# The mLSTM head stage of a two-layer decoder trunk, with the next iteration's projections dealt between its steps

## The chip, the cores and the metric

One NeuronCore of one Trainium2 chip runs the whole program, two layers, in one launch. The metric is device time in microseconds, the median of several executions. One further execution was taken with the hardware profiler, and all rows below come from it.

## What is computed

Each layer adds a token mixer and an expert feed-forward to x (512 tokens by 1024 columns, float32). The mixer has three branches that read column groups of one projection of the normalised x: an RG-LRU, a forgetting attention, and an mLSTM; each is projected, gated and summed ("merged"). The change touches the third branch:

```python
q, k, v = 8 heads of 128 columns each, of xn @ w_in;  i, f = 8 gate columns each
b = cumsum(log_sigmoid(f));  d[t, s] = b[t] - b[s] + i[s] for s <= t;  m[t] = running maximum
w[t, s] = exp(d[t, s] - m[t]) * (q[t] . k[s]) / sqrt(128)
h[t] = sum_s w[t, s] v[s] / max(|sum_s w[t, s]|, exp(-m[t]))
hc = h - mean(h);  y = hc / sqrt(mean(hc * hc) + eps) * norm_w * sigmoid(o)
merged += sigmoid(gate_c) * (y @ w_br_mlstm)
```

## The kernel before

Every dense projection is made with split float32: POOL turns a weight slot of 128 by 1024 (loaded by SP's DMA into one of four ring buffers) into a rounded high part `w_hi` and a remainder `w_lo` (`split_parts`, L610 to L616), each in one of two buffers; TensorE then sums 24 products of 512 columns, 16 with the high activations (L727) and 8 with the low ones (L730), into bank s of four (`project`). ScalarE or VectorE empties the bank. A round is four slots. `proj_done`, `split_ready` and the `drained` semaphores tie them together. Each engine runs its own program strictly in its written order, and waits on semaphores.

A layer goes through LRU, forgetting attention (FQ), values (MV), merge (MB), output gates (MO), then the mLSTM head stage (**MQ**, four iterations), merge (MC), output projection, normalisation, and the experts (UE, VE), which take the second half. In FQ the next round's projection is already dealt between the steps of attention by a generator, `project_beside`: `next()` on it issues `step` products.

An MQ iteration handles two heads, p = 0 and 1. In the kernel before it is a hardware loop (`Fori`) on each engine:

- **TensorE** projects the iteration's queries and keys (slots 0 to 3: q0, k0, q1, k1). After slots 1 and 2 it spreads the gate rows of head 0 and 1 over all partitions (L922; G to bank 6, M to bank 7), with selectors that POOL writes (`sel`, L664). When all four banks are empty: scores of both heads (L931, banks 4 and 5, four key blocks each), numerator and denominator of head 0 (L942), mean of head 0 (L950), numerator and denominator of head 1, then mean square of head 0, mean of head 1, mean square of head 1 (L950).
- **ScalarE** copies queries and keys (L1241), copies G (L1251), makes the floor exp(-m) (L1254) and, behind VectorE's mask, the decays E (L1261, L1263); later the numerator's copy (L1268), squares (L1272, L1237), square roots (L1279), and the high part of y (L1281).
- **VectorE** adds the mask (L1654), multiplies scores into decays (`weigh`, L1664), takes the larger of denominator and floor (L1675, L1677), centres (L1683), adds up the variance (L1700), then for each head reciprocal (L1703) and two products (L1705, L1707), and last the low part of y (`low_part`, L1491).
- **POOL** splits slots 0 and 1, writes `sel`, copies the iteration's two heads of values into a buffer `vst` (L669), from which the numerator's weights are loaded, and splits slots 2 and 3.

`fill_wait` makes TensorE wait until a bank's last contents are taken; `filled` and `drained` count per phase and iteration. The merge MC then runs four rounds; slots 0 and 1 of a round (gates) read xn, slots 2 and 3 read y, so slot 2 of its first round waits for y's low part. `stand` increments a semaphore that nothing waits on.

Of the kernel before, what the change touches and what calls it, by code (L numbers as in the profile page):

```python
# [11 lines left out]
ALU = mybir.AluOpType  # L12
ACT = mybir.ActivationFunctionType
AX = mybir.AxisListType
ds = bass.ds

P = 128
# [131 lines left out]

def build(nc, x_in, w_stream, w_lru, pvec, nrows, fnorm, u_tab, v_tab, out):  # L150
# [3 lines left out]
    with ExitStack() as ctx:  # L154
# [76 lines left out]
        vst = sb("vst", [P, TT, 2, P])  # L231
# [70 lines left out]
        pickw = vst[:, 0, 0, :]  # L302
# [79 lines left out]
        vst_ready = Count(sem("vst_ready"), dict(MQ=(4, 1)))  # L382
# [42 lines left out]
        def loaded(L, phase, i):  # L425
            return 16 * (L * NLOAD + i + LOAD0[phase]) + 16

# [137 lines left out]
        def _(pool):  # L565
# [68 lines left out]
            with pool.Fori(0, DEPTH) as L:  # L634
# [24 lines left out]
                with pool.Fori(0, 4) as i:  # L659
                    split_round(L, "MQ", i, (0, 1))  # L660
                    pool.wait_ge(filled[7].sem, filled[7].at(L, "MQ", i, 0))
                    pool.wait_ge(filled[6].sem, filled[6].at(L, "MQ", i, 0))
                    stand(pool)
                    nc.gpsimd.tensor_copy(sel[:, 0:2, :], head_hot[:, ds(2 * i, 2)]  # L664
                                          .unsqueeze(2).to_broadcast([M_AT + ML_H, 2, P])).then_inc(sel_ready.sem, 1)
                    for s in range(4):
                        pool.wait_ge(drained[s].sem, drained[s].at(L, "MV", 1, 1))
# [3 lines left out]
                    split_round(L, "MQ", i, (2, 3))  # L671
# [27 lines left out]
        def _(pe):  # L699
# [45 lines left out]
            def project_beside(L, ph, i, x, step):  # L745

                for s in range(4):
# [56 lines left out]
            def merge(L, ph, hi, branch_out):  # L804


                stand(pe)
                with pe.Fori(0, 4) as i:
                    for s in range(4):
                        if s == 2:  # L810
                            pe.wait_ge(y_lo_ready.sem, y_lo_ready.at(L, *branch_out, 1))
                        project(L, ph, i, s, x_parts(xl_mix) if s < 2 else y_parts(hi))

            with pe.Fori(0, DEPTH) as L:
# [101 lines left out]
                with pe.Fori(0, 4) as i:  # L916
                    n = {6: 0, 7: 0}

                    def spread(b, p, at):
                        fill_wait(b, L, "MQ", i, n[b])  # L920
# [4 lines left out]
                        n[b] += 1  # L925

                    def scores_of(p):
                        for s in range(TT):
                            b = 4 + s % 2
                            fill_wait(b, L, "MQ", i, 2 * p + s // 2)  # L930
                            nc.tensor.matmul(bank[b][:, 0:SEQ - s * P], qk[:, 2 * p + 1, s * P:(s + 1) * P],  # L931
                                             qk[:, 2 * p, s * P:SEQ], start=True, stop=True)\
                                .then_inc(filled[b].sem, 1)

                    def num_den(p):
                        for b in (6, 7):
                            fill_wait(b, L, "MQ", i, n[b])
                            for s in range(TT):
                                if b == 6:
                                    pe.wait_ge(wts_ready.sem, wts_ready.at(L, "MQ", i, 4 * p + s + 1))  # L940
                                lhsT = vst[:, s, p, :] if b == 6 else ones[:, 0:P]
                                mm = nc.tensor.matmul(bank[b][:, s * P:SEQ], lhsT, E[:, p, s, 0:SEQ - s * P],  # L942
                                                      start=(s == 0), stop=(s == TT - 1))
                            mm.then_inc(filled[b].sem, 1)
                            n[b] += 1

                    def mean(p, b, src, ready):
                        pe.wait_ge(ready.sem, ready.at(L, "MQ", i, p + 1))
                        fill_wait(b, L, "MQ", i, n[b])
                        nc.tensor.matmul(bank[b][:, :], inv[:, :], src[:, p, :], start=True, stop=True)\  # L950
                            .then_inc(filled[b].sem, 1)
                        n[b] += 1


                    for s in range(4):
                        project(L, "MQ", i, s, x_parts(xl_mix))
                        if s == 1:
                            pe.wait_ge(sel_ready.sem, sel_ready.at(L, "MQ", i, 1))
                        if s in (1, 2):
                            spread(6, s - 1, G_AT)  # L960
                            spread(7, s - 1, M_AT)
                    for s in range(4):
                        pe.wait_ge(drained_sem[s], drnd(L, "MQ", i) + 2)
                    pe.wait_ge(vst_ready.sem, vst_ready.at(L, "MQ", i, 1))
                    scores_of(0)
                    scores_of(1)
                    num_den(0)
                    mean(0, 6, hh, h_ready)
                    num_den(1)
                    mean(0, 7, sq, hsq_ready)  # L970
                    mean(1, 6, hh, h_ready)
                    mean(1, 7, sq, hsq_ready)
                merge(L, "MC", y_hi, ("MQ", 3))
# [110 lines left out]
        def _(act):  # L1084
# [39 lines left out]
            with act.Fori(0, DEPTH) as L:  # L1124
# [109 lines left out]
                with act.Fori(0, 4) as i:  # L1234
                    def centred_square(p):
                        act.wait_ge(hc_ready.sem, hc_ready.at(L, "MQ", i, p + 1))
                        nc.scalar.activation(sq[:, p, :], hh[:, p, :], ACT.Square).then_inc(hsq_ready.sem, 1)  # L1237

                    for s in range(4):
                        proj_wait(L, "MQ", i, s)  # L1240
                        nc.scalar.activation(qk[:, s, :], bank[s][:, :], ACT.Copy,  # L1241
                                             scale=ML_D ** -0.5 if s % 2 == 1 else 1.0)\
                            .then_inc(drained_sem[s], 1)
                        if s in (1, 2):

                            p = s - 1
                            act.wait_ge(filled[6].sem, filled[6].at(L, "MQ", i, p + 1))
                            if p == 1:

                                act.wait_ge(dec_ready.sem, dec_ready.at(L, "MQ", i, TT))  # L1250
                            nc.scalar.copy(gb, bank[6][:, :]).then_inc(drained_sem[6], 1)  # L1251
                            act.wait_ge(filled[7].sem, filled[7].at(L, "MQ", i, p + 1))
                            act.wait_ge(ml_y.sem, ml_y.at(L, "MQ", i, p) - 1)
                            nc.scalar.activation(em[:, p, :], bank[7][:, :], ACT.Exp, scale=-1.0)\  # L1254
                                .then_inc(drained_sem[7], 1)
                            act.wait_ge(drained_sem[6], drained[6].at(L, "MQ", i, p + 1))
                            act.wait_ge(gdm_ready.sem, gdm_ready.at(L, "MQ", i, p + 1))
                            for k in range(TT):
                                gs = gcol[:, k, ds(2 * i + p, 1)]
                                if k < TT - 1:  # L1260
                                    nc.scalar.activation(E[:, p, k, P:SEQ - k * P], gb[:, (k + 1) * P:], ACT.Exp,  # L1261
                                                         scale=-1.0, bias=gs)
                                nc.scalar.activation(E[:, p, k, 0:P], gdm[:, k, :], ACT.Exp, scale=-1.0, bias=gs)\  # L1263
                                    .then_inc(dec_ready.sem, 1)
                    for p in range(2):

                        act.wait_ge(filled[6].sem, filled[6].at(L, "MQ", i, 3 + 2 * p))
                        nc.scalar.copy(hh[:, p, :], bank[6][:, :]).then_inc(drained_sem[6], 1)  # L1268
                        act.wait_ge(drained_sem[6], drained[6].at(L, "MQ", i, 3 + 2 * p))
                        act.sem_inc(h_ready.sem, 1)  # L1270
                        act.wait_ge(drained_sem[7], drained[7].at(L, "MQ", i, 3 + p))
                        nc.scalar.activation(em[:, p, :], em[:, p, :], ACT.Square, scale=EPS ** 0.5)\  # L1272
                            .then_inc(dsq_ready.sem, 1)
                        if p == 1:
                            centred_square(0)
# [118 lines left out]
        def _(dve):  # L1394
# [102 lines left out]
            with dve.Fori(0, DEPTH) as L:  # L1497
# [375 lines left out]
                def one_hots(k, s):  # L1873
# [5 lines left out]
                    if k % 8 == 0 and s == 0:  # L1879
                        V.tensor_copy(pickw, pickT[:, 2, :])  # L1880
# [206 lines left out]
```

## Time and profile before

| | us |
|---|---|
| median of 3 runs | 4980.68 |
| lowest, highest | 4971.8, 4984.4 |
| profiled execution | 4974.69 |
| its span | 4972.8 |

Head stages in the profiled span: from 690 to 920 in the first layer, 3170 to 3390 in the second. The profile's chain of waits follows the work that ended last backwards; its pieces, given with a start and a duration, are the work and the waits on which the end depended. In the timeline of an engine, the number in brackets behind a row is the idle time ahead of it and the instruction that ended it. TensorE's products are pipelined, so a product's duration is longer than the spacing to the next. A float32 product that is not split shows as two records.

### The profile page before, as it was taken

The page shows a single profiled execution, that of the slowest core. Times are in us where ns is not written, and L with a number is a line of the kernel's source. Part 1 is how long each engine was busy: PE and PEld are TensorE (multiplying, and loading weights), DVE is VectorE, ACT ScalarE, POOL GpSimd, SP SyncE. Part 2 cuts the span into 40 slices and gives each one's busy share as a digit, 9 for nine tenths or more (in the row PEclk, how much of TensorE's full clock was granted, in tenths as well). Part 3 has the DMA queues.
Part 4 walks back from the last instruction along what each step waited for, and adds up shares of the span by engine and source line. Part 5 has one row for each costly group of instructions (what it writes and reads, how often), then busy time and mean ns, then how long its engine had stood idle before and what let it go on. Part 6 is the DMA issues. An engine that isn't in the chain of part 4 may idle for free.

```text
span 4972.8 us, 73478 instructions
## 1 busy us (share of the span) xinstructions
PE 4465.8 (90%) x21194; PEld 3693.0 (74%) x21194; DVE 3182.8 (64%) x5031; ACT 1763.7 (35%) x3198; POOL 2740.8 (55%) x1485
## 2 busy tenths in 40 slices
PE   6899998889989887999878999989898889879998
PEld 4666775679888886777756667757798888867776
DVE  7434225338889775888883352343488897668888
ACT  2234213213555652333222341231145556523332
POOL 5643664565455664555456436636554566645554
PEclk9999999999999998999989999999999999989999
DMA  2211221224578999999722112212246889989996
GB/s 96 68 60 39 73 76 42 68 76 127 179 243 265 293 303 317 337 341 331 276 67 70 56 39 81 72 42 74 72 141 188 243 263 303 303 301 342 338 331 251
DMA packets 463118, 893.00 MB, mean 180 GB/s; under 512 B 41376, under 2 KB 320416, under 8 KB 459808
## 3 DMA queue, kind: packets, MB, share of 16 engines
q1 hardware_dynamic: 387424, 617.22, 38.4%
q0 software_dynamic: 73728, 268.47, 15.8%
q10 hardware_dynamic: 1728, 4.89, 0.3%
q14 instruction: 180, 1.47, 0.1%
q8 instruction: 58, 0.95, 0.1%
HBM read 787.65 MB, written 102.76 MB: 179 GB/s over the span
## 4 chain that ended last, share of the span: by engine, by line
PE 54%; DVE 19%; DMA 10%; issue 9%; ACT 4%; SPq 2%; DVEq 1%; POOL 1%; ACTq 0%; POOLq 0%
DMA ring<-v_tab 7%; PE pair L727 6%; PE bank L727 6%; PE bank L1062 5%; PE bank L1067 5%; PE bank L1057 4%; PE bank L1005 3%; PE pair L730 3%; PE bank L730 3%; DMA ring<-u_tab 3%; PE bank L880 2%; PE bank L753 2%; DVE ring L1849 2%; PE bank L794 2%; DVE qk L1882 2%
## 5 line engine op out<-in xcount | busy, mean ns | idle before, releaser
L613 POOL TENSOR_TENSOR w_hi<-ring,ones 128x1024 fp32r<-128x1024 f32 x272 | 546.7, 2010 | 857.1 <-PE bank L730 291.3
L601 POOL TENSOR_TENSOR w_lo<-ring,w_hi 128x1024 fp32r<-128x1024 f32 x256 | 634.2, 2478 | 552.3 <-ACT w_hi L1304 545.8
L1005 PE MATMUL bank<-xT,w_hi 128*128 128x384 f32 x2048 | 728.0, 355 | 24.7 <-ACT gst L1316 21.2
L616 POOL TENSOR_TENSOR w_lo<-ring,w_hi 128x1024 fp32r<-128x1024 f32 x272 | 696.9, 2562 | 21.3
L1005 PE MATMUL bank<-xl_peer,w_hi 128*128 128x384 f32 x2048 | 705.3, 344 | 0.0
L1310 ACT CAST w_hi<-ring 128x1024 fp32r<-128x1024 f32 x256 | 269.7, 1053 | 719.5 <-PE bank L1067 440.9
L1304 ACT CAST w_hi<-ring 128x1024 fp32r<-128x1024 f32 x256 | 268.9, 1050 | 637.7 <-DVE ring L1849 496.6
L1941 DVE TENSOR_TENSOR cl<-att,ch 128x384 fp32r<-128x384 f32 x256 | 356.8, 1394 | 213.8 <-ACT ch L1375 206.8
L607 POOL TENSOR_TENSOR w_lo<-ring,w_hi 128x1024 fp32r<-128x1024 f32 x128 | 306.6, 2395 | 316.7 <-ACT w_hi L1310 316.6
L1057 PE MATMUL bank<-w_hi,ch 128*128 128x512 f32 x1536 | 395.4, 393 | 53.4 <-ACT ch L1375 53.3
L1005 PEld LDWEIGHTS bank<-xT,w_hi 128*128 128x128 f32 x2048 | 402.5, 197 | 28.4 <-ACT w_hi L1304 18.8
L1062 PE MATMUL bank<-w_hi,cl 128*128 128x512 f32 x1536 | 396.6, 394 | 20.2 <-DVE cl L1941 19.9
L1005 PEld LDWEIGHTS bank<-xl_peer,w_hi 128*128 128x128 f32 x2048 | 402.1, 196 | 0.3 <-issue 0.3
L1009 PE MATMUL bank<-xT,w_lo 128*128 128x384 f32 x2048 | 398.0, 335 | 0.0
L1067 PE MATMUL bank<-w_lo,ch 128*128 128x512 f32 x1536 | 390.4, 389 | 0.0
L1057 PEld LDWEIGHTS bank<-w_hi,ch 128*128 128x128 f32 x1536 | 287.7, 189 | 122.6 <-ACT w_hi L1310 60.6
L1009 PEld LDWEIGHTS bank<-xT,w_lo 128*128 128x128 f32 x2048 | 359.4, 188 | 0.8 <-POOL w_lo L601 0.8
L1062 PEld LDWEIGHTS bank<-w_hi,cl 128*128 128x128 f32 x1536 | 287.6, 189 | 93.4 <-DVE cl L1941 33.8
L1036 PE MATMUL bank<-qk 128*128 128x128 f32 x1536 | 223.2, 291 | 140.1 <-ACT qk L1332 139.1
L727 PE MATMUL bank<-xT,w_hi 128*128 128x512 f32 (+1 forms) x816 | 329.7, 404 | 17.6 <-POOL w_lo L616 10.4
L1067 PEld LDWEIGHTS bank<-w_lo,ch 128*128 128x128 f32 x1536 | 288.7, 188 | 60.6
L1036 PEld LDWEIGHTS bank<-qk 128*128 128x128 f32 x1536 | 202.9, 200 | 167.1 <-issue 166.7
(322 smaller groups left out, 9184.4 us busy)
## 6 DMA issues: line engine op xcount, KB each, us to landing
ring<-v_tab SPq DMA_DIRECT2D x256, 512.0 KB
ring<-w_stream SPq DMA_DIRECT2D x240, 512.0 KB
ring<-u_tab SPq DMA_DIRECT2D x512, 128.0 KB
g_spill<-gst SPq DMA_DIRECT2D x256, 192.0 KB
hn<-u_tab SPq DMA_DIRECT2D x256, 128.0 KB
x_last<-u_tab SPq DMA_DIRECT2D x256, 128.0 KB
w_spill<-vg SPq DMA_DIRECT2D x12, 2048.0 KB, 8.9
w_spill<-att SPq DMA_DIRECT2D x12, 2048.0 KB
```

Source lines behind the costliest of these rows:

```text
L601: nc.gpsimd.tensor_tensor(w_lo[s % 2][:, :], ring[2 + s % 2][:, :], w_hi[s % 2][:, :].bitcast(F32), ALU.subtract)\
L607: nc.gpsimd.tensor_tensor(w_lo[s % 2][:, :], ring[s][:, :], w_hi[s % 2][:, :].bitcast(F32), ALU.subtract)\
L613: nc.gpsimd.tensor_tensor(w_hi[b][:, 0:n], src, ones[:, 0:1].to_broadcast([P, n]), ALU.mult)\
L616: nc.gpsimd.tensor_tensor(w_lo[b][:, 0:n], src, w_hi[b][:, 0:n].bitcast(F32), ALU.subtract)\
L727: nc.tensor.matmul(out, w(c)[part], x(c)[0], start=(c == 0 and part == 0), stop=False)
L1005: nc.tensor.matmul(out, w_hi[s % 2][:, c * P:(c + 1) * P], dense_parts(c)[part], start=(c == 0 and part == 0), stop=False)
L1009: mm = nc.tensor.matmul(out, w_lo[s % 2][:, c * P:(c + 1) * P], dense_parts(c)[0], start=False, stop=(c == KC - 1))
L1036: mm = nc.tensor.matmul(bank[b][:, j * P:(j + 1) * P], hot2[s % 2][:, j, :], hot1[s % 2][:, j, :], start=True, stop=True)
L1057: nc.tensor.matmul(bank[acc[2 * t + h]][:, :], ch[s % 2][:, cols[t]], w_hi[s % 2][:, halves[h]], start=start, stop=False)
L1062: nc.tensor.matmul(bank[acc[2 * t + h]][:, :], cl[s % 2][:, cols[t]], w_hi[s % 2][:, halves[h]], start=False, stop=False)
L1067: mm = nc.tensor.matmul(bank[acc[2 * t + h]][:, :], ch[s % 2][:, cols[t]], w_lo[s % 2][:, halves[h]], start=False, stop=stop)
L1941: V.tensor_tensor(cl[s % 2][:, :], cf[s % 2], ch[s % 2][:, :].bitcast(F32), ALU.subtract)\
```

## The change

TensorE, ScalarE and POOL run the four iterations unrolled; VectorE runs three in a loop and the last one apart. During iteration i TensorE issues iteration i + 1's projection in pieces of six products (four per slot), and its gate rows singly, between iteration i's steps. In the last iteration the pieces are slots 0 and 1 of MC's first round, and MC then begins with its slots 2 and 3. Counts on banks 6 and 7 follow two written-out lists of fills. ScalarE's and VectorE's steps are put in a new order. The numerator reads its weights from `v_sb` itself; `vst` goes, and `pickw`, which lay in it, gets a buffer of its own.

```diff
+FILLS = {6: ["G00", "G01"], 7: ["M00", "M01"]}
+for _i in range(4):
+    _next = _i < 3
+    FILLS[6] += [f"num{_i}0", f"h{_i}0", f"num{_i}1"] + [f"G{_i + 1}0"] * _next + [f"h{_i}1"] + [f"G{_i + 1}1"] * _next
+    FILLS[7] += [f"den{_i}0", f"den{_i}1", f"q{_i}0", f"q{_i}1"] + [f"M{_i + 1}0", f"M{_i + 1}1"] * _next
...
         @block.gpsimd
-                    nc.gpsimd.tensor_copy(vst[:, :, :, :].rearrange("p t a n -> p t (a n)"),
-                                          v_sb[:, :, ds(2 * P * i, 2 * P)]).then_inc(vst_ready.sem, 1)
...
+                for i in range(1, 4):
+                    pool.wait_ge(filled[6].sem, sums(filled, L, f"G{i - 1}1"))
+                    pool.wait_ge(filled[7].sem, sums(filled, L, f"M{i - 1}1"))
                     stand(pool)
+                    gate_rows(i)
+                    split_round(L, "MQ", i)
...
         @block.tensor
+                            lhsT = v_sb[:, s, at:at + P] if b == 6 else ones[:, 0:P]
...
+                for i in range(4):
+                    if i < 3:
+                        beside = project_beside(L, "MQ", i + 1, x_parts(xl_mix), 6)
+                        share = [4, 2, 2, 2, 3, 3]
+                    else:
+                        beside = project_beside(L, "MC", 0, x_parts(xl_mix), 6, range(2))
+                        share = [4, 1, 1, 1, 1, 0]
+
+                    def dense():
+                        for _ in range(share.pop(0)):
+                            next(beside)
+
+                    scores_of(i, 0)
+                    scores_of(i, 1)
+                    dense()
+                    num_den(i, 0)
+                    dense()
+                    mean(i, 0, f"h{i}0", hh, h_ready)
+                    num_den(i, 1)
+                    dense()
+                    if i < 3:
+                        pe.wait_ge(sel_ready.sem, sel_ready.at(L, "MQ", i + 1, 1))
+                        spread(i + 1, 0)[0]()
+                    dense()
+                    mean(i, 0, f"q{i}0", sq, hsq_ready)
+                    mean(i, 1, f"h{i}1", hh, h_ready)
+                    dense()
+                    mean(i, 1, f"q{i}1", sq, hsq_ready)
+                    if i < 3:
+                        spread(i + 1, 0)[1]()
+                    dense()
+                    if i < 3:
+                        for one in spread(i + 1, 1):
+                            one()
+                    beside.close()
+                merge(L, "MC", y_hi, ("MQ", 3), 1)
...
         @block.scalar
+                for i in range(4):
+                    if i < 3:
+                        query_key(i + 1, 0)
+                    numerator(i, 0)
+                    floor_square(i, 0)
+                    numerator(i, 1)
+                    if i < 3:
+                        query_key(i + 1, 1)
+                        decay_row(i + 1, 0)
+                    centred_square(i, 0)
+                    floor_square(i, 1)
+                    if i < 3:
+                        decays(i + 1, 0)
+                        query_key(i + 1, 2)
+                    centred_square(i, 1)
+                    deviation(i, 0)
+                    deviation(i, 1)
+                    if i < 3:
+                        floors(i + 1, 0)
+                        query_key(i + 1, 3)
+                        decay_row(i + 1, 1)
+                        decays(i + 1, 1)
+                        floors(i + 1, 1)
                     act.wait_ge(ml_y.sem, ml_y.at(L, "MQ", i, 2))
+                    nc.scalar.copy(y_hi[:, 2 * i:2 * i + 2, :], yT[:, 2 * i:2 * i + 2, :]).then_inc(y_hi_ready.sem, 1)
...
         @block.vector
+                decay_mask(0, 0)
+                decay_mask(0, 1)
+                def heads(i, more):
                     c = Chain(dve, dve_step, L, "MQ", i)
+                    weigh(i, 0)
+                    weigh(i, 1)
+                    denominator(c, i, 0)
+                    centre(i, 0)
+                    denominator(c, i, 1)
+                    if more:
+                        decay_mask(i + 1, 0)
+                    centre(i, 1)
+                    variance(i, 0)
+                    variance(i, 1)
                     for p in range(2):
                         dve.wait_ge(dev_ready.sem, dev_ready.at(L, "MQ", i, p + 1))
                         c.step(V.reciprocal(em[:, p, :], em[:, p, :]))
...
+                    if more:
+                        decay_mask(i + 1, 1)
                     c.close()
                     low_part(L, "MQ", i, y_lo, yT, y_hi, 1)
...
+                with dve.Fori(0, 3) as i:
+                    heads(i, True)
+                heads(3, False)
```

`numerator`, `floor_square`, `centred_square`, `deviation`, `decay_row`, `decays`, `floors` and `query_key` are the same instructions as before, each now a function. `floors(i + 1, p)` waits until y of head p of iteration i is done, `decays` for the mask, `decay_row` of head 1 for head 0's decays.

## Rows read from the trace of the kernel before

**Rows 1.** The page: busy time of each engine, with share and instructions
```profile
PE 4465.8 (90%) x21194; PEld 3693.0 (74%) x21194; DVE 3182.8 (64%) x5031; ACT 1763.7 (35%) x3198; POOL 2740.8 (55%) x1485
```

**Rows 2.** Windows: busy us by engine, then PEclk, DMA share, GB/s
```profile
769.67:823.11 53.44, 44.02 (x161) 28.89 (x161) 26.11 (x25) 17.40 (x33) 19.76 (x11) 0.97 0.12 39
823.11:877.59 54.48, 45.31 (x161) 29.45 (x161) 26.11 (x25) 17.41 (x33) 19.74 (x11) 0.94 0.11 40
877.59:920.49 42.90, 32.65 (x105) 20.09 (x105) 22.38 (x23) 9.38 (x13) 9.98 (x5) 0.92 0.08 30
...
925.00:960.00 35.00, 35.00 (x155) 29.01 (x154) 11.84 (x10) 4.76 (x5) 27.23 (x12) 1.00 0.27 90
```

**Rows 3.** Chain of waits: start, us, what; last row in the second layer
```profile
776.76 4.34 PE bank L942 x16
...
783.27 4.59 PE bank L942 x16
...
790.62 1.99 PE bank L950 x4
...
794.47 1.14 PE bank L950 x2
...
796.33 3.35 DVE att L1703
...
805.58 2.55 DVE big L1707
...
831.25 4.34 PE bank L942 x16
...
3388.28 1.55 DVE y_lo L1491
```

**Rows 4.** Timeline of VectorE across the loop's end
```profile
800.59 0.69 DVE L1707 TENSOR_TENSOR big<-att,vg 128x512 f32 x1 [0.19 <-DVE att L1705]
...
809.43 1.86 DVE L1491 TENSOR_TENSOR y_lo<-big,y_hi  x1 [1.31 <-ACT y_hi L1281]
812.22 1.89 DVE L1654 TENSOR_TENSOR att<-att,mask_k 128x512 f32<-128x512 f32 x1 [0.93 <-ACT att L1251]
...
825.38 0.69 DVE L1664 TENSOR_TENSOR att<-bank,att 128x512 f32<-128x512 f32 x1 [5.80 <-PE bank L931]
```

**Rows 5.** Chain of waits: two slots in a row of the merge MC
```profile
954.99 3.63 PE bank L727 x16
960.43 3.63 PE bank L727 x16
```

**Rows 6.** Timeline of TensorE: a pair of gate rows spread
```profile
808.06 0.73 PE L922 MATMUL bank<-row_parts,sel 8*128 8x512 f32 x4
```

**Rows 7.** Timeline of ScalarE: y's high part, and the last decays of head 0
```profile
808.26 1.05 ACT L1281 CAST y_hi<-big  x1 [11.18 <-DVE big L1707]
...
816.11 0.68 ACT L1263 ACTIVATE att<-att,gcol 128x128 f32<-128x128 f32 x2
```

**Rows 8.** Timeline of VectorE at the stage's end
```profile
914.53 2.54 DVE L1707 TENSOR_TENSOR big<-att,vg 128x512 f32 x1 [0.26 <-DVE att L1705]
```

**Rows 9.** Timeline of POOL: value copy and splits
```profile
796.39 1.04 POOL L669 COPY vst<-vg 128x1024 f32 x1
802.87 1.90 POOL L613 TENSOR_TENSOR w_hi<-ring,ones 128x1024 fp32r<-128x1024 f32 x1 [5.44 <-PE bank L730]
804.85 2.72 POOL L616 TENSOR_TENSOR w_lo<-ring,w_hi 128x1024 fp32r<-128x1024 f32 x1
808.31 1.90 POOL L613 TENSOR_TENSOR w_hi<-ring,ones 128x1024 fp32r<-128x1024 f32 x1 [0.74 <-PE bank L730]
810.28 3.27 POOL L616 TENSOR_TENSOR w_lo<-ring,w_hi 128x1024 fp32r<-128x1024 f32 x1
```

**Rows 10.** Windows of 2 us in the two falls of the clock
```profile
796.00:798.00 2.00, 2.00 (x6) 1.52 (x6) 2.00 (x2) 0.63 (x1) 1.42 (x2) 0.50 0.00 0
...
824.00:826.00 2.00, 2.00 (x4) 0.67 (x2) 0.62 (x1) 0.00 (x0) 1.33 (x1) 0.50 0.00 0
```

More of the change, by code:

```diff
@@ L802, in xl_of_tile, with merge @@
                 return xl_mix[:, t, c * P:(c + 1) * P]
-            def merge(L, ph, hi, branch_out):
+            def merge(L, ph, hi, branch_out, begun=0):
+                if begun:
+                    pe.wait_ge(y_lo_ready.sem, y_lo_ready.at(L, *branch_out, 1))
+                    for s in range(2, 4):
+                        project(L, ph, 0, s, y_parts(hi))
                 stand(pe)
-                with pe.Fori(0, 4) as i:
+                with pe.Fori(begun, 4) as i:
                     for s in range(4):
-                        if s == 2:
+                        if s == 2 and not begun:
                             pe.wait_ge(y_lo_ready.sem, y_lo_ready.at(L, *branch_out, 1))
@@ L935, in num_den @@
[L935 to L961, printed above, removed]
@@ L973, in _, with scores_of @@
-                merge(L, "MC", y_hi, ("MQ", 3))
+                    return (lambda: one(f"G{i}{p}", G_AT)), (lambda: one(f"M{i}{p}", M_AT))
+                def scores_of(i, p):
+                    for s in (2 * p, 2 * p + 1):
+                        pe.wait_ge(drained_sem[s], drnd(L, "MQ", i) + 2)
+                    for s in range(TT):
+                        b = 4 + s % 2
+                        fill_wait(b, L, "MQ", i, 2 * p + s // 2)
+                        nc.tensor.matmul(bank[b][:, 0:SEQ - s * P], qk[:, 2 * p + 1, s * P:(s + 1) * P],
+                                         qk[:, 2 * p, s * P:SEQ], start=True, stop=True)\
+                            .then_inc(filled[b].sem, 1)
@@ new lines, in mean @@
+                def mean(i, p, name, src, ready):
+                    b = FILL[name]
+                    pe.wait_ge(ready.sem, ready.at(L, "MQ", i, p + 1))
+                    sum_wait(name)
+                    nc.tensor.matmul(bank[b][:, :], inv[:, :], src[:, p, :], start=True, stop=True)\
+                        .then_inc(filled[b].sem, 1)
+                for s in range(4):
+                    project(L, "MQ", 0, s, x_parts(xl_mix))
+                    if s == 1:
+                        pe.wait_ge(sel_ready.sem, sel_ready.at(L, "MQ", 0, 1))
+                    if s in (1, 2):
+                        for one in spread(0, s - 1):
+                            one()
@@ L1232, in _ @@
                             .then_inc(drained_sem[s], 1)
[L1234 to L1275, printed above, removed]
-                    centred_square(1)
-                    for p in range(2):
-                        act.wait_ge(drained_sem[7], drained[7].at(L, "MQ", i, 5 + p))
-                        nc.scalar.activation(em[:, p, :], em[:, p, :], ACT.Sqrt).then_inc(dev_ready.sem, 1)
@@ new lines, in deviation @@
+                def deviation(i, p):
+                    act.wait_ge(drained_sem[7], sums(drained, L, f"q{i}{p}"))
+                    nc.scalar.activation(em[:, p, :], em[:, p, :], ACT.Sqrt).then_inc(dev_ready.sem, 1)
+                for s in range(4):
+                    query_key(0, s)
+                    if s in (1, 2):
+                        decay_row(0, s - 1)
+                        floors(0, s - 1)
+                        decays(0, s - 1)
+                for i in range(4):
[21 more added lines that the diff above has]
+                        floors(i + 1, 1)
```

187 lines of the change are left out of this document (107 added, 80 removed).

## The prediction

> **What bounds the kernel now.** The page's totals first [rows 1]: TensorE is busy for 90% of the span, so hiding other work behind it, or filling its holes, looks like the only way on. But the share is an average. The window table of the head stage [rows 2] gives TensorE 44 to 45 us of work in each full iteration of 53.4 to 54.5 us (two of three are shown), at a granted clock of 0.94 to 0.97, and 32.7 of 42.9 us in the last one, while the merge behind it is full (35.00 of 35.00). So each layer has some 9 us of holes per iteration, which the change wants to fill.
>
> What closes an iteration is read in the chain of waits [rows 3]. I count from one iteration's first numerator group (776.76) to the next (831.25): 54.49 us. Numerator and denominator of head 0 take 4.34 us; its mean and centring bring head 1's numerator to 783.27; its groups end 4.59 us later. The next means start at 790.62 (2.76 us after those groups end, waiting for the floor and centred squares), the last variance at 794.47 (1.86 us after the means end). Then VectorE: reciprocal at 796.33, y of head 1 complete at 805.58 + 2.55 = 808.13. From there to the next iteration's first weighing product, 825.38 [rows 4], pass 17.25 us: y's high part, a table load, queries and keys, both heads' masks and decays. Another 5.87 us of scores and weighing reach the next numerator. This is a loop through three engines, and **TensorE is not its limit**. Only the first two projections of an iteration are hidden now: they begin right after the last variance, under the reciprocals.
>
> **The change, part by part.**
> *Dealt pieces.* A slot's projection is 24 products, 5.44 us (960.43 - 954.99 [rows 5]); a piece is a quarter, 1.36 us. In iterations 0 to 2 the shares are 4, 2, 2, 2, 3, 3. TensorE takes its work in order, so a piece is free only where it already waited. Ahead of head 0's numerator: 4 pieces, 5.44 us, and no wait there (the chain goes from the weighing's scores straight into the numerator): +5.44. Ahead of head 0's mean: 2 pieces, no wait: +2.72. Between head 1's denominator and the next means: 2 + 2 pieces and one gate row, half the 0.73 us pair plus some 0.1 of issue, 0.45 [rows 6]: 5.89 against a wait of 2.76: +3.13. Ahead of the last variance: 3 pieces, 4.08, against 1.86: +2.22. The last 3 pieces lie behind it, under the reciprocals, at nothing; without that cover they would be 4.08. The loop's first part is **13.5 us longer**.
> *What leaves the loop.* Queries, keys and head 0's mask and decays of the next iteration are done before y is ready, so the 17.25 us go.
> *What stands in their place.* Here the new order on VectorE matters. `decay_mask(i + 1, 1)` is put behind both heads' final products, and `low_part` behind that, ahead of the next `weigh`. `low_part` waits for `y_hi`, and ScalarE makes `y_hi` only after `decays(i + 1, 1)` and `floors(i + 1, 1)`, which wait for that very mask. So after y: mask, decays, floor, y high, y low, and only then the weighing, on which scores, numerators and all TensorE work queue up. The mask is 0.69 us (a product of the same width without contention [rows 4]) to 1.89 (now); I take 0.69, as POOL may be between splits. Decays with the hand-over: 814.11 to 816.79, 2.7 [rows 4, 7]. Floor 0.5 net, high part 1.05 with 0.13 before it [rows 7]. Low part 1.55 (second layer) to 1.86 [rows 3, 4], I take 1.55, with its 0.12 wait and 0.35 of issue behind it. Sum 7.1.
> Steady iteration: +13.5 - 17.25 + 7.1 = **+3.4**, three per layer: +10.2.
> *Last iteration.* Its shares are 4, 1, 1, 1, 1, 0, the merge's two x-side slots, which now hide under the final reciprocals. +5.44, then +1.36; 2.72 against the 2.76 wait and 1.36 against the 1.86, at nothing: +6.8. At its end no split is left beside VectorE: the last product at 914.53 took 2.54 against 0.69, and y's low part can go from 1.86 to 1.55 [rows 3, 4, 8]; 2.2 comes off, and some 0.5 of issue. About **+4.1**. The merge's y-side slots start at the same distance from y low as now (920.49).
> *Values in place.* The 1.04 us copy and its semaphore go from POOL [rows 9]. POOL stood idle 5.44 us right behind it, so nothing is gained; if POOL were the limit it would be worth 4 us a layer. Weight loads from the value tensor have the same 128 columns: nothing, below and above, since a load is shorter than its product.
> *POOL and SP.* The copy of gate-row selectors now needs the previous gate rows spread, and a round's splits (1.90 + 2.72 us each [rows 9]) start only then. The first is needed by the first piece, behind mask, decays and weighing: nothing. The weight loads keep their order, and the DMA share is 0.08 to 0.12 [rows 2]: nothing.
> *Unrolled loops.* The chain shows no loop cost at the present boundary, 0 to 0.5 us per iteration: nothing.
> Sum: 10.2 + 4.1 = 14.3 per layer, 28.6 for both. The profiled execution took 4974.7 us (span 4972.8), so 5003.3. The median shown lies 6.0 above that execution, which lies within the spread of the three runs (12.6), so I leave the sum: **5003 us**. No later stage can take the delay back: experts wait for the whole mixer.
>
> **The shared port.** VectorE's product at 805.58 took 2.55 us while POOL's low split ran from 804.85 to 807.57; it ended 0.56 us after the split. Y low at 809.43 ended 1.08 us after the high split, whose successor (810.28) took 3.27 although the low split before it took 2.72 with no such product ahead of it [rows 3, 4, 9]. So one instruction waits for the other's end. The Trainium skill ("SBUF — State Buffer", section "SBUF: two separate sides") has it that the two share a port pair under an exclusive lock, held for the whole instruction by whichever starts first. By that rule, the trace agrees. By it the mask just behind y meets a split each time, since the gate rows release POOL shortly before: the sum would be 7 us larger.
>
> **Rivals.**
> *B, slower still (0.15).* TensorE now stands for some 11 us between the last gate rows and the weighing. After its holes today the granted clock is 0.50 from 796 to 798 and again from 824 to 826 [rows 10], 1.2 GHz instead of 2.4: each such 2 us lose 1 us, the first beside the reciprocals, the second on the path. With longer holes scores and the first 4 pieces run at 1.2 GHz, on the path: up to +2 per iteration, 12 in all. With the port met at mask and low part each time (1.2 + 0.3, 9 in all) and 2 more of hand-overs per iteration it reaches 5035.
> *C, nothing to measure (0.22).* The 13.5 and the 10.2 saved are near each other. If the 4 pieces ahead of the numerator cost half (the pieces running while the last weighing products are still under way) the steady iteration comes to +0.7 and the whole to 4974.7 + 2 x (2.1 + 4.1 - 2.7) = 4982.
> *D, faster (0.13).* If y's high and low parts are not what VectorE waits for at the loop's end, the weighing starts when TensorE's pieces are through, and TensorE's work sets the period, about 44.5 us [rows 2]: -10 per iteration, +4 at the end, -52 in all, 4923. For it speaks that all holes are on offer; against it the order written out on VectorE and ScalarE. It decides at the 7.1 us behind y: under 3.7 the iteration gains, and D needs them gone. That the change leaves the order as it was (pieces run late, at the loop's end) would be C.
>
> **Numbers.** Forecast 0.50 (its own range 4992 to 5013). About 0.3% (15 us) is what this kernel's measurement can tell from none. Slower by more: 0.43 of the forecast (its upper part and middle) and 0.15 of B, and 0.02 of C: 0.60. Within: 0.07 of the forecast, 0.19 of C: 0.27 with 0.01 of D. Faster: 0.12 of D and 0.01 of C: 0.13. The range takes in forecast, C and B and leaves D out: 4979 to 5035.
>
> **What would show it.** In the profile after: numerator to numerator 57 to 58.5 us in three iterations, against 54.5; behind y the row of mask, decays, floor, y high and y low, over 6 us, on the chain; TensorE idle about 11 us before the third score group, released by VectorE's weighing; TensorE full from there to the last variance. POOL must not appear as a releaser of the pieces. From the last iteration's first score to the merge's third slot, 42.9 now: longer by the 4 us and by the wait that the scores then have for the weighing. If the period is under 50, low part or mask was not on the path and D holds; if it is 60, the clock and the port.

## The result and the profile after

| | before | after |
|---|---|---|
| median | 4982.54 us (6 runs) | 5011.76 us (6 runs) |
| lowest, highest | 4969.7, 4992.33 | 4988.7, 5015.31 |
| ratio, 95% interval | | 1.0055, 1.0031 to 1.0079 |
| profiled execution, span | 4972.8 | 5009.5 |

The change makes the kernel slower by 29 us; 5003 was forecast, 29 above the profiled execution before. The page's totals hardly differ from [rows 1]:

```profile
PE 4475.7 (89%) x21194; PEld 3698.9 (74%) x21194; DVE 3181.2 (64%) x5031; ACT 1763.7 (35%) x3196; POOL 2728.4 (54%) x1477
```

The same work is done in a longer time, so one looks for waits. The chain of waits of the kernel after, from the second iteration's numerators to the next iteration's (L975 is the numerator and denominator, before L942; L774 a dealt piece, before none; L983 the means, before L950; L1804 and L1806 the reciprocal and its product, L1750 the mask, L1376 y's high part, L1760 the weighing, L962 the scores):

```profile
786.06 4.32 PE bank L975 x16
790.37 2.77 PE bank L774 x12
793.14 0.87 PE bank L983 x2
...
794.86 4.58 PE bank L975 x16
799.43 2.76 PE bank L774 x12
...
802.85 2.94 PE pair L774 x12
805.79 1.72 PE bank L983 x4
807.51 4.12 PE pair L774 x18
811.63 1.06 PE bank L983 x2
...
813.50 3.27 DVE att L1804
...
826.76 2.39 DVE att L1750
...
832.13 0.94 ACT y_hi L1376
834.33 0.69 DVE att L1760
...
836.90 4.80 PE bank L962 x8
841.70 5.48 PE bank L774 x24
847.18 4.31 PE bank L975 x16
```

This is the loop of [rows 3] with the dealt pieces in it. Numerator to numerator it takes 847.18 - 786.06 = 61.1 us, against 54.5. Before, only waits and short steps of other engines stood between the product groups of L942, the means and the variances; now every such place has an L774 row, and the reciprocal starts 27.4 us after the start of the numerators (before: 796.33 - 776.76 = 19.6). The end of the loop is shorter, but not by as much. Added up for this iteration against the one of [rows 3]: four pieces ahead of the numerator 5.5, numerator to reciprocal 7.9, reciprocal to y 1.5 (13.3 for 11.8), y to weighing -9.8 (7.5 for 17.25), scores and weighing 1.5 (7.4 for 5.9), together the 6.6 us. VectorE's timeline there, and ScalarE's and POOL's beside it, in the kernel after:

```profile
821.67 2.43 DVE L1806 TENSOR_TENSOR att<-att 128x512 f32<-128x512 f32 x1
824.36 2.48 DVE L1808 TENSOR_TENSOR big<-att,vg 128x512 f32 x1 [0.26 <-DVE att L1806]
826.76 2.38 DVE L1750 TENSOR_TENSOR att<-att,mask_k 128x512 f32<-128x512 f32 x1
833.19 1.22 DVE L1586 TENSOR_TENSOR y_lo<-big,y_hi  x1 [4.04 <-ACT y_hi L1376]
834.33 0.68 DVE L1760 TENSOR_TENSOR att<-bank,att 128x512 f32<-128x512 f32 x1
```

```profile
829.18 0.61 ACT L1309 ACTIVATE att<-att,gcol 128x384 f32<-128x384 f32 x1 [7.86 <-DVE att L1750]
...
831.56 0.57 ACT L1321 ACTIVATE att<-bank 128x512 f32<-128x512 f32 x1
832.04 1.03 ACT L1376 CAST y_hi<-big 128x1024 fp32r<-128x1024 f32 x1
```

```profile
821.66 1.89 POOL L630 TENSOR_TENSOR w_hi<-ring,ones 128x1024 fp32r<-128x1024 f32 x1
823.63 2.67 POOL L633 TENSOR_TENSOR w_lo<-ring,w_hi 128x1024 fp32r<-128x1024 f32 x1
826.26 2.34 POOL L630 TENSOR_TENSOR w_hi<-ring,ones 128x1024 fp32r<-128x1024 f32 x1
828.67 2.67 POOL L633 TENSOR_TENSOR w_lo<-ring,w_hi 128x1024 fp32r<-128x1024 f32 x1
```

Behind y come mask, decays, floor (L1321), y high, y low and only then the weighing, in the order forecast; VectorE stands idle for 4.04 us ahead of y low. Three VectorE rows in a row take 2.4 us where 0.69 is their length alone, while POOL's splits run, and each ends just behind the end of a split: at 824.10, 826.84 and 829.14, the splits at 823.55, 826.30 and 828.60. The windows of the kernel after, cut at each iteration's first weighing product (columns as in [rows 2], whose cuts lie at the first score product):

```profile
773.42:834.33 60.91, 47.32 (x160) 29.87 (x160) 27.03 (x26) 17.52 (x33) 18.74 (x9) 0.86 0.11 35
834.33:891.52 57.19, 47.26 (x160) 29.89 (x160) 23.13 (x26) 17.51 (x33) 17.36 (x8) 0.89 0.12 38
891.52:935.82 44.30, 29.20 (x100) 18.36 (x100) 19.97 (x24) 8.54 (x11) 8.49 (x4) 0.85 0.07 24
```

TensorE's holes are larger than before (13.6 us against 9), and its granted clock is 0.86 to 0.89 where it was 0.94 to 0.97.

### The profile page after: what moved, and what is told of

It is laid out like the page before. It is cut to its first block, busy times and chain, and to the rows that moved or that the text cites. A ratio compares the mean times of both kernels' runs of the same rounds, so it can differ in the third digit from the quotient of the medians.

```text
span 5009.5 us, 73238 instructions
## 1 busy us (share of the span) xinstructions
PE 4475.7 (89%) x21194; PEld 3698.9 (74%) x21194; DVE 3181.2 (64%) x5031; ACT 1763.7 (35%) x3196; POOL 2728.4 (54%) x1477
## 4 chain that ended last, share of the span: by engine, by line
PE 56%; DVE 17%; DMA 10%; issue 10%; ACT 3%; SPq 2%; POOL 1%; DVEq 1%; ACTq 0%; another core or an unknown queue 0%; POOLq 0%
DMA ring<-v_tab 6%; PE pair L748 6%; PE bank L748 6%; PE bank L1117 5%; PE bank L1122 4%; PE bank L1112 4%; PE bank L774 3%; PE bank L1060 3%; DMA ring<-u_tab 3%; PE pair L751 3%; PE bank L751 3%; PE pair L774 2%; PE bank L905 2%; PE bank L815 2%; DVE ring L1955 2%
## 5 line engine op out<-in xcount | busy, mean ns | idle before, releaser
L1117 PE MATMUL bank<-w_hi,cl 128*128 128x512 f32 x1536 | 396.3, 393 | 19.8 <-DVE cl L2047 19.6
L1988 DVE TENSOR_TENSOR qk<-bank,iota_k 128x512 f32<-128x512 f32 x384 | 244.0, 676 | 84.1 <-PE bank L1091 62.2
```

The costliest lines, as they stand in the source:

```text
L1117: nc.tensor.matmul(bank[acc[2 * t + h]][:, :], cl[s % 2][:, cols[t]], w_hi[s % 2][:, halves[h]], start=False, stop=False)
```

## The experiments

All start from the kernel after, but for experiments 7 and 8. Ratios are to the kernel before, timed beside each experiment; differences in us are to the changed kernel's median of 5011.8. The kernel before had medians of 4981.7 to 4984.1 us beside the experiments, so such a difference is uncertain by some 2 us for that alone. An edit shifts line numbers a little: the row that reads `mask_k` is the mask, the two rows behind a reciprocal are the products that make y, `y_lo` is y's low part. A period is numerator to numerator.

**1. Y's low part off the loop.**
```diff
                     weigh(i, 1)
+                    if not more:
+                        with dve.Fori(0, 3) as j:
+                            low_part(L, "MQ", j, y_lo, yT, y_hi, 1)
...
-                    low_part(L, "MQ", i, y_lo, yT, y_hi, 1)
+                    if not more:
+                        low_part(L, "MQ", i, y_lo, yT, y_hi, 1)
```


> The changed kernel, with y's low parts of iterations 0 to 2 made behind the last iteration's weighing instead of ahead of the next weighing. Chain theory (the loop's end is mask, decays, floor, y high, y low, weighing): the weighing can start when the decays are done, 2.7 us earlier per steady iteration; numerator to numerator in the first layer from 60.9, 61.1, 56.7 to about 58.2, 58.4, 54, and some 16 us off the whole. Rival (TensorE's own work sets the period): nothing moves. Rival (port and clock make the delay): at most the low part's own 1.2 us, 7 in all.

Measured: 4981.95 us, ratio 1.0001 (0.9990 to 1.0013), 29.8 us faster than the changed kernel and level with the one before. The direction is the chain theory's, the size is twice it. VectorE's timeline of this run shows why:

```profile
819.99 2.38 DVE L1750 TENSOR_TENSOR att<-att,mask_k 128x512 f32<-128x512 f32 x1
822.28 0.68 DVE L1760 TENSOR_TENSOR att<-bank,att 128x512 f32<-128x512 f32 x1
```

The weighing follows the mask at once. Head 0's decays were ready long before; only head 1's hang on this mask, and this run makes them while head 0 is weighed. So the low part, by waiting for y high behind the decays, had held the weighing for everything between mask and weighing, 834.33 - 829.14 = 5.2 us, not for the 2.7 that I wrote. Numerator to numerator: 55.3, 55.2, 51.3 us. Taking a single instruction of 1.2 us, which nobody needed before the merge, off the loop is worth as much as the whole loss. It is not the only such term: experiments 3 and 4 give back 20 and 49 us, so what each gives back is the worth of its own edit and not a share of the 29.

**2. The mask earlier.**
```diff
                         c.wait()
+                        if more and p:
+                            decay_mask(i + 1, 1)
                         c.step(V.tensor_tensor(hh[:, p, :], hh[:, p, :], em[:, p, :], ALU.mult))
...
-                    if more:
-                        decay_mask(i + 1, 1)
```


> The changed kernel, with head 1's mask of the next iteration put between head 1's reciprocal and its two products, so that ScalarE makes the decays during the products. Chain theory: 2.7 us of decays leave the loop's end in each steady iteration, some 16 us in all; the mask itself only changes place. Rival (TensorE sets the period): nothing. Rival (port): the mask meets a split at its new place too, nothing gained from that part, and 16 us is a ceiling.

Measured: 5001.85 us, ratio 1.0044 (1.0031 to 1.0056), 9.9 us faster. The decays leave the path, but the mask at its new place and both products meet the splits:

```profile
819.71 2.29 DVE L1750 TENSOR_TENSOR att<-att,mask_k 128x512 f32<-128x512 f32 x1 [0.17 <-DVE att L1804]
821.92 2.83 DVE L1808 TENSOR_TENSOR att<-att 128x512 f32<-128x512 f32 x1
825.00 2.04 DVE L1810 TENSOR_TENSOR big<-att,vg 128x512 f32 x1 [0.26 <-DVE att L1808]
828.80 1.53 DVE L1586 TENSOR_TENSOR y_lo<-big,y_hi  x1 [1.75 <-ACT y_hi L1376]
```

The wait ahead of y low falls from 4.04 to 1.75 us, its length grows from 1.22 to 1.53. The ceiling of 16 held.

**3. The splits held back until the mask is done.**
```diff
                     gate_rows(i)
+                    pool.wait_ge(gdm_ready.sem, gdm_ready.at(L, "MQ", i - 1, 2))
+                    stand(pool)
                     split_round(L, "MQ", i)
```


> The changed kernel, with POOL's splits of a round held back until head 1's mask is done. Port theory: head 1's two products and the mask, now 2.43, 2.48 and 2.38 us, take 0.7 each; 4 to 5 us off each of the first two iterations and 1 to 2 off the third, some 20 us in all, less up to 1.2 us where y's low part then meets a split. The pieces must not wait: their first split is ready 9 us after the mask. Rival (the three products are long for another reason): they keep 2.4 us and nothing changes.

Measured: 4991.66 us, ratio 1.0017 (1.0005 to 1.0029), 20.1 us faster, as expected for the whole. The profiled execution is the slowest of its ten (5002.8), so its rows and periods are read here, not its span. In the first two iterations the three rows have their own length, and y low meets a split (1.80 against 1.22):

```profile
817.46 0.69 DVE L1808 TENSOR_TENSOR att<-att 128x512 f32<-128x512 f32 x1
818.41 0.69 DVE L1810 TENSOR_TENSOR big<-att,vg 128x512 f32 x1 [0.26 <-DVE att L1808]
819.02 0.68 DVE L1752 TENSOR_TENSOR att<-att,mask_k 128x512 f32<-128x512 f32 x1
823.75 1.80 DVE L1588 TENSOR_TENSOR y_lo<-big,y_hi  x1 [4.05 <-ACT y_hi L1378]
...
822.12 2.35 POOL L633 TENSOR_TENSOR w_lo<-ring,w_hi 128x1024 fp32r<-128x1024 f32 x1
824.43 2.87 POOL L630 TENSOR_TENSOR w_hi<-ring,ones 128x1024 fp32r<-128x1024 f32 x1
```

The first-layer periods are 55.9, 56.2 and 56.5, where they were 60.9, 61.1 and 56.7. The third had mostly escaped already (its mask took 0.69), and the 1 to 2 us expected of it did not come: the one product that meets a split there took 2.02 in the changed kernel and 2.01 here, since that split belongs to the merge's round, which the edit doesn't hold back. The mechanism that the prediction had put into rival B is real, and without it the changed kernel gets back two thirds of its loss.

**4. The four pieces ahead of the numerator moved to the end.**
```diff
-                        share = [4, 2, 2, 2, 3, 3]
+                        share = [0, 2, 2, 2, 3, 7]
...
-                        share = [4, 1, 1, 1, 1, 0]
+                        share = [0, 1, 1, 1, 1, 4]
```
ScalarE's `query_key(i + 1, 0)` goes behind `numerator(i, 1)`, slots 1 and 2 behind `deviation(i, 1)` and `floors(i + 1, 0)`.

> The changed kernel, with the four pieces ahead of head 0's numerator given to the last place behind the variances (shares 0, 2, 2, 2, 3, 7 and 0, 1, 1, 1, 1, 4; ScalarE's key and query copies moved to fit). Chain theory: TensorE stands idle at the loop's end, so the pieces are free there, and 5.4 us leave each of the four iterations: 43 us in all, about 4968, faster than the kernel before. Rival (TensorE's own work sets the period): they come back at the end, and nothing changes. Rival (clock): the gain is larger by up to 1.5 us an iteration, as the hole in TensorE gets shorter.

Measured: 4963.05 us, ratio 0.9962 (0.9950 to 0.9974), 48.7 us faster than the changed kernel and 19 faster than the kernel before. The periods fall from 61 to 53.5 and 53.8, by 7.4 and not 5.4. VectorE's timeline shows what came on top, and what was given back:

```profile
808.66 0.69 DVE L1805 TENSOR_TENSOR att<-att 128x512 f32<-128x512 f32 x1
809.62 0.69 DVE L1807 TENSOR_TENSOR big<-att,vg 128x512 f32 x1 [0.26 <-DVE att L1805]
812.45 2.31 DVE L1749 TENSOR_TENSOR att<-att,mask_k 128x512 f32<-128x512 f32 x1 [2.14 <-ACT att L1300]
```

TensorE now reaches the gate rows of head 1 later, so POOL's splits start later and both products are free of them (3.5 us); but the mask waits 2.14 us for the row's copy (L1300), which ScalarE makes behind the last key copy. 5.5 + 3.5 - 2.1 is 6.9; the other 0.5 is not taken apart (scores and weighing, 7.1 us for 7.4 at a granted clock of 0.60 for 0.51, are part of it). At the end the pieces cost TensorE nothing that the period shows.

**5 and 6. TensorE kept busy through the hole.**
```diff
                         fill_wait(b, L, "MQ", i, 2 * p + s // 2)
+                        for _ in range(10 if i and p == 0 and s == 0 else 0):
+                            nc.tensor.matmul(bank[b][:, 0:SEQ], qk[:, 1, 0:P], qk[:, 0, 0:SEQ], start=True, stop=True)
```
The bank is overwritten by the true product behind them. The second run has 14 in place of 10.

> The changed kernel, with the first score product of iterations 1 to 3 made ten more times into its own bank (it is overwritten each time), so that TensorE works through the hole ahead of the weighing. Clock theory: the scores and the first piece run at full clock, the stretch from the first weighing product to the end of the scores goes from 6.6 us to 5.3, and 1.3 to 1.5 us leave each of three iterations, 8 to 9 us in all. The ten products (some 8.5 us at full clock, the hole is 11.8) must end ahead of the weighing. Rival (the clock costs nothing that matters): no change. If they end late, slower.

Measured: 5003.96 us, ratio 1.0051 (1.0033 to 1.0068), 7.8 us below the changed kernel's median. The two intervals (that of the changed kernel is 1.0031 to 1.0079) overlap almost wholly, so no gain is shown by the times. The windows of this run separate two iterations. In the first TensorE stood idle for 3.66 us until the weighing, the granted clock fell to 0.50 and the period stayed at 60.9. In the second it stood idle for 1.99 us, the clock was 1.00 at the scores, and the period was 59.5; but there the extra products had begun at 0.50 (820 to 822) and lasted 10.5 us for 8.9, which is why they reached so far:

```profile
770.00:774.00 4.00, 1.03 (x3) 0.60 (x3) 2.38 (x3) 0.96 (x2) 0.00 (x0) 0.75 0.00 0
774.00:778.00 4.00, 3.91 (x8) 1.84 (x8) 1.41 (x3) 0.00 (x0) 0.00 (x0) 0.50 0.00 0
...
832.00:836.00 4.00, 1.67 (x5) 0.89 (x6) 3.00 (x5) 0.00 (x0) 0.00 (x0) 1.00 0.00 0
836.00:840.00 4.00, 3.61 (x14) 2.07 (x13) 2.03 (x5) 0.00 (x0) 0.00 (x0) 1.00 0.00 0
```

> As keep_busy, with fourteen extra products instead of ten. There they ended 3.7 us ahead of the weighing and the clock fell again in one of two iterations looked at; that iteration kept 60.9 us, the other fell to 59.5. Clock theory: with the hole filled, both of the first two iterations take 59.3 to 59.5 and the third about 56, and some 9 us are off the whole against the changed kernel, about 5002. Rival (the clock is not what stretched the scores): the first stays at 60.9. If the products run past the weighing's start, the periods grow by up to 1 us.

Measured: 5013.09 us, ratio 1.0061 (1.0047 to 1.0076): no gain. The clock fell as the fourteen products began (0.50 from 762 to 764), they lasted 13.9 us and ran past the moment when VectorE was free; it waited 1.7 us for the scores. All three periods are 61.2 to 61.3 us: the third, whose hole was only 7.0 us, grew by 4.5, more than the 1 us that had been allowed for. But the clock then was 1.00, and from the first weighing product (775.37) to the dealt pieces (781.14) passed 5.8 us, against 834.33 to 841.70, 7.4 us at a granted clock of 0.51, in the changed kernel. So the clock's price on the scores, 1.6 us in this iteration, is shown in the trace; as a saving of the whole kernel it was not reached. The two windows, that of the changed kernel first:

```profile
834.33:841.70 7.37, 6.54 (x13) 3.43 (x14) 3.63 (x8) 0.00 (x0) 0.00 (x0) 0.51 0.00 0
...
775.37:781.14 5.77, 4.59 (x15) 2.06 (x14) 3.45 (x7) 0.00 (x0) 0.00 (x0) 1.00 0.00 0
```

**7 and 8. The kernel before, unrolled; and reading values in place.** `unroll_only` replaces TensorE's `pe.Fori(0, 4)` by a Python loop in the kernel before. `in_place` does that, and:
```diff
-                                lhsT = vst[:, s, p, :] if b == 6 else ones[:, 0:P]
+                                lhsT = v_sb[:, s, 2 * P * i + P * p:2 * P * i + P * p + P] if b == 6 else ones[:, 0:P]
```
with POOL's copy and its waits gone. (With the loop kept, the weights' address would be in a register, so the two can't be parted the other way.)

> The kernel before, with TensorE's head-stage loop unrolled, the numerator's weights read from the value tensor itself and POOL's copy gone; nothing dealt. The prediction costed both at nothing: no change within 0.15%, POOL's idle time ahead of the third slot's split grows by the copy's 1.04 us. Rival (the copy held back the splits): up to 4 us a layer faster. Rival (unrolled code costs loading): some us slower, with idle TensorE time that nothing released.

> The kernel before with TensorE's head-stage loop unrolled and nothing else; POOL's copy and the value buffer stay. It splits in_place's 8.5 us. If the missing copy brought them: the same time as the kernel before, within 0.1%. If the unrolled loop did (its instructions reach the scores in time, or change when the clock falls): 6 to 10 us faster, 4974 to 4978, and more of the six periods at 51.7 us instead of 54.3. If it was chance in the clock: in between, with an interval over zero.

Measured: in_place 4973.21 us, ratio 0.9983 (0.9971 to 0.9996); unroll_only 4972.48 us, ratio 0.9981 (0.9971 to 0.9991). The two are the same, so the missing copy is worth nothing, as costed; POOL's idle time ahead of the next split grew from 5.44 to 6.47 us in its place. The unrolled kernel is some 9 us faster, which had been costed at nothing. Where they lie isn't settled: the profile of in_place has three periods of six at 51.7 us and the others at 54.1 to 54.4, but it is of its fastest execution, 14 us below its median. That of unroll_only has one of six, as the kernel before has, so the sign that was to show the unrolled loop at work is missing. Its head stages are no shorter: the six stretches from first weighing to first weighing add up to 322.9 us, before 323.2. What is shorter lies in code that the edit leaves alone, 7.5 us of it behind the second layer's last y low (1575.5 us to the end, before 1583.0). Over all the profiles that stretch goes from 1572.7 to 1585.9, so two spans can differ by several us for reasons outside the head stage; lengths inside the stage are the safer comparison.

**9. Low part off the loop and the four pieces moved.** The edits of 1 and 4 together.

> low_late and four_later together. If the two costs lie one behind the other on one loop, they add: 5.6 us of low_late leave each of six iterations of four_later (53.5 us each), some 33 us, about 4930, periods near 48. Rival (TensorE, or the last key copy behind its last piece, already holds the mask back in four_later): less than half of that.

Measured: 4933.68 us, ratio 0.9909 (0.9883 to 0.9934); periods 48.1, 48.0, 46.3. They add: 78.1 us below the changed kernel, against 29.8 and 48.7 apart. The rival, by which the late key copy would swallow most of it, falls.

**10. Pieces where TensorE waited, the rest behind the variances.** TensorE's order, with shares 1, 2, 2, 2, 4, 5 (last iteration 1, 2, 5). All lines behind the scores are shown as new, those that were there before too:
```diff
+                    num_den(i, 0)
+                    mean(i, 0, f"h{i}0", hh, h_ready)
+                    dense()
+                    num_den(i, 1)
+                    dense()
+                    mean(i, 0, f"q{i}0", sq, hsq_ready)
+                    mean(i, 1, f"h{i}1", hh, h_ready)
+                    dense()
+                    mean(i, 1, f"q{i}1", sq, hsq_ready)
+                    if i < 3:
+                        pe.wait_ge(sel_ready.sem, sel_ready.at(L, "MQ", i + 1, 1))
+                        spread(i + 1, 0)[0]()
+                        dense()
+                        spread(i + 1, 0)[1]()
+                        dense()
+                        for one in spread(i + 1, 1):
+                            one()
+                        dense()
```
All of ScalarE's copies, floors and decays of the next iteration go behind the square roots, head by head; VectorE makes each head's mask right behind that head's y; low parts as in experiment 1; the list of fills of bank 6 is reordered to match.

> The changed kernel re-ordered: pieces only where TensorE waited before (1 for head 0's centring, 2 ahead of the next means, 2 ahead of the last mean square), the other 11 behind it with the gate rows between them; each head's mask right behind its own y; low parts as in low_late. Chain theory: the loop of waits is then shorter than TensorE's work, and that work sets the period: 21.8 for pieces, some 6 scores, 8.9 numerators and denominators, 4 means, 2 gate rows, 43 to 45 us against 54.4 before; with an unchanged last iteration some 30 us a layer, 60 in all, about 4920. Rival (the waits of ScalarE between copies and decays hold the scores back): 48 to 50 us, 4945 to 4955.

Measured: 4910.42 us, ratio 0.9860 (0.9840 to 0.9880), the fastest kernel here: 101 us below the changed one, 72 to 74 below the one before. Its windows, cut at the second and third numerators:

```profile
763.12:806.78 43.66, 42.48 (x161) 28.03 (x161) 20.64 (x25) 17.63 (x33) 17.83 (x9) 1.00 0.14 48
```

TensorE works 42.5 of 43.7 us at a granted clock of 1.00, so next to no holes are left: here its own work sets the period. In experiment 9 it still had 4.2 us of holes in 48.0, in the changed kernel 13.6.

## Why the prediction was right

By its own steps, against the first layer of the trace after:

- *The dealt pieces lengthen the loop.* Right. From numerator to reciprocal 8.07 us were to be added to the 19.57, making 27.64; measured 27.44 in both first iterations. The four pieces ahead of the numerator: 5.44 forecast, 5.48 measured. Experiments 4 and 10 take them away and get them back.
- *What stands behind y.* The order was right: mask, decays, floor, y high, y low, weighing. 7.1 us forecast; measured 826.84 to 834.33, 7.5, in the first two iterations and 5.9 in the third. The agreement in the first two is two errors that nearly cancel: from y to the mask's end 2.3 us for 0.69, and all that follows 5.2 for 6.4 (y low 1.22 for 1.55, with next to no issue behind it).
- *The steady iteration, +3.4.* Mis-sized. Periods of 60.9, 61.1 and 56.7 us were measured where 57.9 came out of the sum. First, y's two products met POOL's splits (reciprocal to y: 13.3 us for 11.8), and so did the mask (+1.7). The sum took 11.8 over from the kernel before and gave the mask its bare length. Second, scores and weighing took 7.4 us for 5.9, at half the clock, after TensorE stood for 10.7 us ahead of them (12.2 and 7.0 in the others). Both had been put into rival B, at its top: +9 for the port at mask and low part, +12 for the clock; of the products beside splits nothing was said. The trace has some 3 us an iteration for the port in two of three, and 1.5 for the clock. So the forecast's mechanism was right, and the terms for mask and products, and for scores and weighing, were too small: part of B's price belonged into the sum.
- *The last iteration, +4.1.* Right: first weighing to the end of y low took 44.3 us, against 40.4. In the second layer it was 44.6 against 39.1, 5.5 more.
- *Left out.* Scores of head 0 no longer wait for all four slots, so the first weighing comes 24.8 us after the stage's first projection begins, not 26.1: 1.3 us a layer gained.
- *Values in place, POOL, SP: nothing.* Right for the copy (experiments 7 and 8) and the weight loads. Wrong for POOL: the split's new place was weighed only by whether pieces wait for it, which they don't, and not by what it runs beside. *Unrolling, nothing*: not borne out, 9 us in the kernel before. The changed kernel is unrolled too; if the gain is in it as well, the rest of the change costs more than 29 us, but no run shows that.

For the first layer: -1.3 + 14.6 + 3.9 = 17.2 us. The second layer was 20.8 slower, as the kernel before had had one period of 51.8 there, and with the longer last iteration. That is 38 in the profiled pair (spans: 36.7), 29 between the medians, and 28.6 in the sum. The sum lies in the interval of the ratio (15 to 39 us); that it met the median so closely is luck, as two terms of it were too small by some 3 and 1.5 us in most iterations, and the profiled pair, from whose rows it was worked out, differs by 8 us more.

On the port, VectorE's three rows of 2.4 us beside POOL's splits and 0.69 us without them (experiment 3) show the whole of it: an instruction waits for the other engine's to end. It holds the other way too: in experiment 3 the split at 824.43, begun while y low ran (823.75 to 825.55), took 2.87 us for 1.89. The Trainium skill's rule ("SBUF — State Buffer", section "SBUF: two separate sides"), an exclusive lock held for a whole instruction, would have made the sum 7 us larger through the mask alone; by that rule, the trace agrees: the mask was 1.7 us longer in four iterations of six, 6.8 in all. Applied also to y's products, it would have given most of the 20 us that experiment 3 got back.

Rival D, TensorE's work as the bound, was wrong for this change for the reason given, the order on VectorE. It was right for what lay within reach: with that order mended and the pieces moved, experiment 10 is where D said, and a little beyond (4910 against 4923; 43.7 us an iteration against 44.5). Rival C falls with the interval.

## What to carry to other kernels

Filling an engine's idle time pays only where the filler sits in a wait. Put ahead of an instruction that the loop depends on, it costs its full length (here 5.5 us an iteration), however empty the engine is elsewhere. When a loop is pipelined by hand, follow the loop through every engine's written order: one short instruction that nobody needs yet (y's low part), queued ahead of the next iteration's first step, can hold all of it. And when work of an engine off the path is moved, ask whom it will run beside.

## What the runs showed that had not been expected

Unrolled code is not neutral here: unrolling TensorE's four iterations and nothing else made the kernel before 0.19% faster (0.9981, 0.9971 to 0.9991), with no wait in the head stage of the profile that it removes; the cause is open. And TensorE's clock could not simply be bought with filler. Behind ten extra products TensorE stood idle for 3.7 us, and the clock was at 0.50 again at the scores (774 to 778). With fourteen it was 1.00 there, but they overran: VectorE waited 1.7 us for the scores, about the 1.6 us that the clock gave back, and the third iteration, which had the smallest hole, lost 4.5.
